# Sample tokens' attention to cached pages, moved from the expert loop to the input projection

## The reference, cut to what matters

```python
p = rmsnorm(x, norm1) @ w_in        # split into q, k, v (attention), q/k/v of the delta rule, z, b, a
q, k = rmsnorm(q), rmsnorm(k)       # 4 heads, 2 parts of 64
s = q . k * 64**-0.5 - slope * |distance|           # masked
w = softmax(s)[part 0] - lam * softmax(s)[part 1]
oa = w @ v                          # prompt: over the prompt; sample: over 1024 cached positions + its own
ob = gated_delta_rule(conv(...))    # 64-token chunks, state carried
x = x + concat(rmsnorm(oa), rmsnorm(ob) * silu(z)) @ w_out
h = rmsnorm(x, norm2); q = h @ peer_wq; choose 16 of 128x128 experts for each of 8 heads
x = x + sum_k gate_k * gelu(h . u[e_k]) * v[e_k]    # 128 expert rows for every token
```

## Time and profile before

| | us |
|---|---|
| three runs | 2112.43, 2114.84, 2120.7 |
| median | 2114.84 |
| the profiled execution | 2114.1 |
| its span, first to last instruction | 2112.3 |
| PE busy | 1779.3 (84%) |
| DVE busy | 1330.4 (63%) |
| ACT busy | 801.4 (38%) |
| POOL busy | 740.7 (35%) |
| DMA | 773.26 MB, mean 366 GB/s |

### The profile page before, as it was taken

How to read it: one execution, slowest core, us unless ns; L and a number is a source line. 1 busy time by engine, 2 the same in 40 slices (tenths; PEclk the granted TensorE clock), 3 DMA queues, 4 the chain that set the end, 5 groups by cost and what they waited for, 6 DMA issues and landing times.

```text
span 2112.3 us, 20529 instructions
## 1 busy us (share of the span) xinstructions
PE 1779.3 (84%) x6195; PEld 885.2 (42%) x6195; DVE 1330.4 (63%) x3021; ACT 801.4 (38%) x2386; POOL 740.7 (35%) x638
## 2 busy tenths in 40 slices
PE   8899999889888798968778897879688799776777
PEld 3345454645344444534444543445233333442111
DVE  2661434489765699766578887567664554569554
ACT  2432222254452356344334646324333322323433
POOL 1210011234444453534434363443322233444442
PEclk9999999999898999989999999979899899989999
DMA  9682312699999999999999999999999999999998
GB/s 306 229 297 75 115 44 90 241 410 426 405 426 428 427 426 426 414 428 407 428 426 426 399 419 422 424 426 427 420 344 412 379 404 393 428 427 427 427 428 334
DMA packets 139817, 773.26 MB, mean 366 GB/s; under 512 B 14641, under 2 KB 23617, under 8 KB 62122
## 3 DMA queue, kind: packets, MB, share of 16 engines
q0 software_dynamic: 83232, 604.52, 68.7%
q1 hardware_dynamic: 52994, 160.12, 20.2%
q10 hardware_dynamic: 3480, 7.31, 1.0%
HBM read 755.91 MB, written 16.26 MB: 366 GB/s over the span
## 4 chain that ended last, share of the span: by engine, by line
PE 42%; DMA 29%; DVE 12%; ACT 8%; issue 5%; POOL 3%; SPq 1%; ACTq 0%; DVEq 0%; POOLq 0%
DMA sb_uv<-in_peer_uv,sb_eidx 23%; PE bank L2061 19%; PE bank L1687 5%; DVE sb_uv L1666 5%; PE bank L2028 3%; PE bank L1962 3%; DMA sb_zone<-in_cache_kT 2%; PE bank L1996 2%; PE bank L1941 2%; POOL sb_uv L906 1%; ACT sb_diag L1263 1%; ACT sb_ew L1256 1%; DMA sb_zone<-in_w_route 1%; POOL sb_brs L849 1%; PE bank L1796 1%
## 5 line engine op out<-in xcount | busy, mean ns | idle before, releaser
L2061 PE MATMUL bank<-sb_uv,sb_diag 128*128 128x512 f32 (+1 forms) x1860 | 942.7, 642 | 250.2 <-ACT sb_diag L1263 239.7
L906 POOL DMA_INDIRECT sb_uv<-in_peer_uv,sb_eidx x576 | 672.8, 1168 | 1010.6 <-PE bank L2061 810.4
L1666 DVE CUSTOM_DVE_ANT_0 sb_uv<-sb_uv,sb_xn 128x1024 f32<-128x1024 f32 x576 | 697.2, 1220 | 282.6 <-DMA sb_uv<-in_peer_uv,sb_eidx 281.3
L2061 PEld LDWEIGHTS bank<-sb_uv,sb_diag 128*128 128x128 f32 (+1 forms) x1860 | 331.1, 193 | 729.4 <-ACT sb_diag L1263 393.5
L1252 ACT ACTIVATE sb_gel<-sb_h 128x1 f32<-128x1 f32 x576 | 116.0, 201 | 796.6 <-DVE sb_h L1666 793.0
L1687 PE MATMUL bank<-sb_w,sb_xnT 128*128 128x512 f32 (+1 forms) x560 | 258.5, 609 | 18.4 <-DVE sb_xnT L1281 8.3
L1263 ACT ACTIVATE sb_diag<-sb_stay,sb_ew 128x128 f32<-128x128 f32 (+1 forms) x465 | 183.2, 394 | 46.5 <-PE bank L2061 2.7
L1640 DVE SCALAR_TENSOR_TENSOR sb_hres<-sb_uv,sb_ew,sb_hres 128x1024 f32<-128x1024 f32 x111 | 142.3, 1282 | 61.4 <-ACT sb_ew L1256 61.3
L1256 ACT ACTIVATE sb_ew<-sb_gel,sb_gate 128x1 f32<-128x1 f32 x576 | 169.6, 294 | 20.3
L2028 PEld LDWEIGHTS bank<-sb_rT,sb_zone 128*128 128x128 f32 x1280 | 156.1, 196 | 28.6 <-issue 28.3
L2028 PE MATMUL bank<-sb_rT,sb_zone 128*128 128x128 f32 x1280 | 157.4, 279 | 2.0 <-issue 1.8
(11 more groups left out here) (321 smaller groups left out, 1528.9 us busy)
## 6 DMA issues: line engine op xcount, KB each, us to landing
sb_zone<-in_w_route SPq DMA_DIRECT2D x20, 2304.0 KB, 12.0
sb_zone<-in_w_mixer SPq DMA_DIRECT2D x10, 2048.0 KB, 12.1
sb_zone<-in_cache_kT SPq DMA_DIRECT2D x64, 256.0 KB, 8.8
sb_zone<-in_cache_v SPq DMA_DIRECT2D x64, 256.0 KB, 15.3
sb_w<-in_w_sections SPq DMA_DIRECT2D x28, 512.0 KB, 5.4
sb_uv<-in_peer_uv,sb_eidx POOLq DMA_INDIRECT x576, 13.6
sb_hres<-pre_conv SPq DMA_DIRECT2D x4, 1024.0 KB
sb_zone<-pre_conv SPq DMA_DIRECT2D x4, 1024.0 KB, 6.2
```

What stands on the lines that cost most here:

```text
L906: nc.gpsimd.indirect_dma_start(uv[:, m % RING, :], None, i["peer_uv"], bass.IndirectOffsetOnAxis(ap=eidx[:, t % 2, n:n + 1], axis=0)).then ...
L1666: nc.vector.tensor_tensor_reduce(out=uv[:, m % RING, 0:D], in0=uv[:, m % RING, 0:D], in1=xn2[:, t % 2, :], scale=1.0, scalar=0.0, op0=ALU. ...
L2061: ins = nc.tensor.matmul(bank[half][0:rows, :], lhsT=G["diag"][:, d % DIAGS, 0:rows], rhs=uv[:, m % RING, D + 512 * half:D + 512 * half + ...
```

## The change

The past attention leaves the expert loop. It now runs between the first units of the projection.

- **Order of units.** `VISITS` starts with the sections v, k, q for tile 4 alone, then come the conv and z sections for all five tiles, then v, k, q for the four prompt tiles. There are still 35 units, but the weights of v, k and q are loaded twice (40 piece loads in place of 28).
- **Place.** `past_at(p, k)` is now 64 + 26 p + k on the scale of the first stage. The units 4 to 14 are due every 10.4, units 15 to 32 every 12.1; `gdn(0)` is due at 182 (was 133), `gdn(1)` at 284 (was 231).
- **Column groups.** Queries are spread over 32 columns for each head, and the four heads write partitions 0, 32, 64 and 96 of one bank; the values go by (half, sequence) to the same four groups; the group changes from one product to the next. The small columns alternate between two groups, with an addition on DVE.
- **Page buffers.** Six quarters of 1 MB: two in the place of the sample states (whose load waits for the last pair), two in `zone`, one in `vtok`, one in `kT`. Keys are issued by SP (`key_loads`), values by POOL (`value_loads`).
- **Other places** for scores, fold matrix, weights and biases; the biases, the tables and the page table are loaded in the first stage; tiles 0 to 3 of the tokens are loaded later (about 29 in place of 0). The norm of the sample outputs (`sample_out_squares`, `sample_out_rstd`, `sample_out_norm`) follows the last pair, and `gdn(0)` waits for it (`s_oa`). In the loop only `mix(PT)` is left for tile 4, with its `w_mixer` load waiting for the scores of tile 3.

```diff
-UNITS = [(g, t) for g in range(NSEC) for t in ORDER]
-Z0, V0, K0 = 3 * NT, 4 * NT, 5 * NT
-LATE = K0 + NT + 3
+VISITS = [(4, [PT]), (5, [PT]), (6, [PT])] + [(g, ORDER) for g in range(4)] + [(g, list(range(PT))) for g in range(4, NSEC)]
+UNITS = [(g, t, v) for v, (g, tiles) in enumerate(VISITS) for t in tiles]
+LAST_OF = [max(n for n, unit in enumerate(UNITS) if unit[2] == v) for v in range(len(VISITS))]
+C0 = 3
+Z0 = C0 + 3 * NT
+V0 = Z0 + NT
...
 def unit_len(n):
-    return 6.9 if n < Z0 else 11.1 if n < LATE else 9.0
+    return 6.9 if n < 4 else 10.4 if n < 15 else 12.1 if n < LATE else 9.0
 
 
 def unit_at(n):
-    if n < Z0:
-        return early_at(22 + 6.9 * n + (10 if n >= NT else 0))
+    if n < 4:
+        return early_at(22 + 6.9 * n)
+    if n < 15:
+        return early_at(55 + 10.4 * (n - 4))
     if n < LATE:
-        return early_at(135 + 11.1 * (n - Z0))
+        return early_at(169.4 + 12.1 * (n - 15))
     return -77 + 9.0 * (n - LATE)
 
...
 def gdn_at(u, k):
     if u < 2:
-        return early_at((133, 231)[u] + (2.06, 2.15)[u] * k)
+        return early_at((182, 284)[u] + (2.06, 2.15)[u] * k)
     return SLOTS * (u - 2) + 11.5 + 0.85 * k
 
...
+    return early_at(64 + 26 * p + k)
 
 
...
+        def load_of(p, values, half, seq):
+            return 8 * p + 4 * values + 2 * half + seq
+
+        def cache_quarter(k):
+
+            b = k % PAGE_BUFFERS
+            if b < 2:
+                return F["sS"][:, 2 * b:2 * b + 2, :, :].rearrange("p h b k -> p (h b k)").rearrange("p (g n) -> p g n", g=4)
+            if b < 4:
...
-                        yield early_at(110 + 9 * h)
+                        yield past_at(NPAIR, 1 + 3 * h)
+                        sp.wait_ge(s_dpv, NPAIR)
                         sp.dma_start(F["sS"][:, h, :, :], i["state_ssm"][0, :, h].rearrange("b v k -> v b k")).then_inc(s_sS, 16)
 
...
-                        n = NT * g - 1
+                    for piece in range(4 * len(VISITS)):
...
-                            sp.wait_ge(s_proj, 4 * n + part - 1)
+                            n, used = LAST_OF[(piece - PIECES) // 4], (piece - PIECES) % 4 + 1
+                            yield unit_at(n) + 0.25 * used * unit_len(n)
+                            sp.wait_ge(s_proj, 4 * n + used)
                         sp.dma_start(F["w"][:, piece % PIECES, :, :].rearrange("p k n -> p (k n)"), i["w_sections"][g][:, quarter_k * part:quarter_k * (part + 1)]).then_inc(s_w[piece % PIECES], 16)
...
+                def key_loads(p):
+                    for half in range(2):
+                        yield (past_at(p - 1, (4.2, 21.5)[half]) if p else early_at(40 + half))
+                        if p == 0:
+                            sp.wait_ge(s_vecs, 112)
+                            sp.wait_ge(s_xnT, 2)
+                        for seq in range(2):
+                            k = load_of(p, 0, half, seq)
+                            pages = []
+                            for g in range(4):
+                                n = (2 * p + seq) * NPG + 4 * half + g
+                                pages.append(sp.value_load(F["pages"][0:1, n:n + 1], min_val=0, max_val=i["cache_kT"].shape[0] - 1))
+                            if p and half == 0:
+                                sp.wait_ge(s_ds, 2 * p)
+                            elif p:
+                                sp.wait_ge(s_dpv, p)
+                            for g in range(4):
+                                sp.dma_start(cache_quarter(k)[:, g, :], i["cache_kT"][bass.ds(pages[g], 1)].rearrange("g p n -> (g p) n")).then_inc(s_keys[half], 16)
 
...
+                def value_loads(p):
+                    for half in range(2):
+                        yield past_at(p, 2.3) if half else past_at(p - 1, 21.6) if p else early_at(42)
+                        if p == 0 and half == 0:
+                            pool.wait_ge(s_vecs, 112)
+                        for seq in range(2):
+                            k = load_of(p, 1, half, seq)
+                            pages = []
+                            for g in range(4):
+                                n = (2 * p + seq) * NPG + 4 * half + g
+                                pages.append(pool.value_load(F["pages"][0:1, n:n + 1], min_val=0, max_val=i["cache_v"].shape[0] - 1))
+                            if half:
+                                pool.wait_ge(s_ds, 2 * p + 1)
+                            elif p:
+                                pool.wait_ge(s_dpv, p)
+                            for g in range(4):
+                                pool.dma_start(cache_quarter(k)[:, g, :], i["cache_v"][bass.ds(pages[g], 1)].rearrange("g p n -> (g p) n")).then_inc(s_vals, 16)
...
+                    for kk in range(0, KC, 2):
+                        for r in range(2):
+                            nc.tensor.matmul(bank[2][32 * r:32 * r + 2 * NH, :], lhsT=F["wba"][:, kk + r, :], rhs=F["xnT"][:, 0:KC * SEQ].rearrange("p (t k r) -> p t k r", t=PT, k=KC)[:, :, kk + r, :], start=kk == 0, stop=kk == KC - 2)
+                        for r in range(2):
+                            ins = nc.tensor.matmul(bank[3][32 * r:32 * r + 2 * NH, 0:LAST], lhsT=F["wba"][:, kk + r, :], rhs=xT(PT)[:, kk + r, :], start=kk == 0, stop=kk == KC - 2)
                     ins.then_inc(s_bap, 1)
-                    yield early_at(75)
...
                 def past(p):
...
+                    for half in range(2):
+                        yield past_at(p, (0, 4)[half])
+                        pe.wait_ge(s_keys[half], 16 + 128 * (p + 1))
+                        if half == 0:
+                            pe.wait_ge(s_qd, 4 * (p + 1))
                             if p:
                                 pe.wait_ge(s_dadd, 4 * p)
+                            else:
+                                pe.wait_ge(s_bad, 2)
+                        for seq in range(2):
+                            for h in range(NH):
+                                ins = nc.tensor.matmul(bank[2 + half][32 * h:32 * h + 32, :].rearrange("p (g k) -> p g k", g=4), lhsT=Qd[:, h, 32 * seq:32 * seq + 32],
+                                                       rhs=cache_quarter(load_of(p, 0, half, seq))[:, :, h * PAGE:(h + 1) * PAGE], start=seq == 0, stop=seq == 1)
                         if half:
...
+                            for seq in range(2):
+                                for h in range(NH):
+                                    ins = nc.tensor.matmul(bank[4][32 * h:32 * h + 32, 0:NSAMP], lhsT=Qd[:, h, 32 * seq:32 * seq + 32], rhs=kT[:, h, NPOS:TOK], start=seq == 0, stop=seq == 1)
                         ins.then_inc(s_ds, 1)
...
+                    yield past_at(p, 15)
                     pe.wait_ge(s_dn, 3 * (p + 1))
                     if p:
                         pe.wait_ge(s_dwc, 2 * p)
+                        pe.wait_ge(s_gatea, 6)
+                    else:
+                        pe.wait_ge(s_bac, 3)
                     for g in range(NPG):
...
+                        nc.tensor.matmul(bank[5][:, 64 * g:64 * g + 64], lhsT=past_S[:, g * PAGE:(g + 1) * PAGE], rhs=past_fold, start=True, stop=True)
+                    nc.tensor.matmul(bank[6][0:NSAMP, 0:64], lhsT=past_S[:, PAST:], rhs=past_fold, start=True, stop=True).then_inc(s_dw, 1)
+                    yield past_at(p, 19.5)
+                    pe.wait_ge(s_dwc, 2 * (p + 1))
+                    if p:
+                        pe.wait_ge(s_doc, p)
+                    pe.wait_ge(s_vals, 256 * (p + 1))
+                    for g in range(4):
+                        for half in range(2):
+                            for seq in range(2):
+                                at = 64 * (4 * half + g) + 32 * seq
+                                r0 = 64 * half + 32 * seq
+                                nc.tensor.matmul(bank[7][r0:r0 + 32, :], lhsT=past_wT[:, at:at + 32], rhs=cache_quarter(load_of(p, 1, half, seq))[:, g, :], start=g == 0, stop=half == 0 and g == 3)
+                    for seq in range(2):
+                        r0 = 64 + 32 * seq
+                        ins = nc.tensor.matmul(bank[7][r0:r0 + 32, :], lhsT=past_wTn[0:NSAMP, 32 * seq:32 * seq + 32], rhs=vtok[0:NSAMP, PT, :], start=False, stop=True)
+                    ins.then_inc(s_dpv, 1)
+                    if p % 2:
+                        yield past_at(p, 26.2)
+                        pe.wait_ge(s_doc, p + 1)
+                        r0 = NSAMP + 32 * (p // 2)
+                        for h in range(NH):
+                            for odd in range(2):
+                                at = 128 * odd + 32 * h
+                                ins = nc.tensor.matmul(bank[6][r0:r0 + 32, h * HD:(h + 1) * HD], lhsT=ea("pick")[:, at:at + 32], rhs=osamp[:, odd, h * HD:(h + 1) * HD], start=odd == 0, stop=odd == 1)
                         ins.then_inc(s_dot, 1)
 ```

555 lines of the change are left out of this document (270 added, 285 removed).

## The result

The changed kernel takes 2131.03 us (median of 10 runs, 2122.24 to 2142.42) against 2114.6 for the kernel before on the same chip: 1.0077 times as long, 95% interval 1.0058 to 1.0096. The prediction was 2080; it missed by 51 us, and by the sign. The profiled execution has a span of 2125.5 us, 13.2 more than before.

The account below looks back on a forecast made before the run. PE was taken to bound the stage before the first gather, the DMA engines the expert loop. From 2114.1 us, 100 less in the loop and 66 more in the first stage (42 + 2 + 22) gave 2080 us, range 2054 to 2108.

Parts of the forecast that it names:

- Part 1: Expert loop, tile 3 to tile 4 output projection: pages and bias tables leave, 433 us become 333, so 100 us go.
- Rival (d): Expert loop: it gives back only the page bytes' 79 us; 2101 us in all, chance 0.03.
- Part 2: PE in the first stage: past attention adds 42 us, with four column groups working side by side at a quarter.
- rival (c): First stage: column groups don't work side by side, 90 us more of PE; 2148 us, chance 0.12.
- Part 3: Gaps at the start of the first stage: idle PE less saved waits for convolution copies, net 2 us, bounds -5 and 10.
- Part 4: DMA engines in the first stage: 201 us of transfers hold `gdn(0)` to 202, 22 us after PE could start it.
- I cost all these at nothing beyond the 22: First stage: units, weight pieces, convolution loads, spills and norm powers standing behind waits add nothing to the DMA term's 22 us.
- Their loss of cover would show in the pair's chain: First stage: spreads, biases, exp and copies on ACT and DVE are hidden; any loss stays within the bound of 48 us.
- rival (b): First stage: waits pile up pair by pair, the DMA term is 48 us and not 22; 2106 us, chance 0.18.
- the pace of 0.11: Sign of being right: eight score or value instructions in a row pace at about 0.11 us and not 0.43.
- the stretch of 333: Sign of being right: the loop's tile-4 stretch falls from 433 to about 333 us at 420 GB/s or more.
- `gdn(0)` at 202: Sign of being right: the transposes of `gdn(0)` in the first stage start at about 202 us.

Follow-up runs that it names:

- groups in the loop: Kernel before, past attention left in the expert loop, the two sequences' products taken in turn, page quarters loaded 0, 2, 1, 3: 2131.1 us, 1.0093 of the kernel before.
- fill runs: Changed kernel with 25 useless products on PE in the places of four waits: 1.0037 and again 1.0039 of the kernel before.
- later fold: Changed kernel with pairs due every 34 us, fold 19.4 in place of 15 after the pair's start, values later too: 2116.5 us, 1.0021 of the kernel before.

## Why the prediction was wrong, step by step

**Bounds of the kernel, Part 1: size right, reason half wrong.** -100 was forecast, -104.5 measured, 96.7 for all behind the first stage. But the dips of the earlier trace rows were put down to PE's serial products; with 52 us fewer of these (groups in the loop) the stretch did not shrink and waits for key pages of 50.3 us stood in it, though that edit changed the order of the loads too. Rival (d) is out.

**Part 2: right.** 42 us were forecast, 40 measured at full clock (44 by the three parts). Four instructions of values start together every 0.43 us:

```profile
101.40 0.59 PE L2049 MATMUL bank<-sb_vtok,sb_zg 128*32 128x512 f32 x1
101.40 0.59 PE L2049 MATMUL bank<-sb_kT,sb_zg 128*32 128x512 f32 x1
101.40 0.60 PE L2049 MATMUL bank<-sb_sS,sb_zg 128*32 128x512 f32 x2
101.83 0.59 PE L2049 MATMUL bank<-sb_vtok,sb_zg 128*32 128x512 f32 x1
```

Against 0.432 us for one instruction that is a factor of 4.0, so rival (c) is out. The Trainium skill ("TensorE: Matmul & The Clock Gate", Measured speedup vs the span model) has 2.38 for three column groups, by which the long products would have cost 7 us more than the sum took. The trace doesn't agree, and the measurement decides: 4.0 for long rows of float32 products over four groups.

**Part 3: too low.** 2 us were forecast; the waits for weight pieces (14.9) and spread queries (5.1), less the 5.7 of the earlier trace rows, are 14. The three sections of weights for one tile each are wanted faster than they land at a DMA share of 0.98.

**Part 4: size right, reason half wrong.** Waits for key pages are 19.7 us for 22. While PE waits for them, the engines are full:

```profile
110.00:120.00 10.00, 7.58 (x29) 2.43 (x27) 2.76 (x5) 4.08 (x15) 4.29 (x8) 1.00 1.02 393
160.00:170.00 10.00, 1.32 (x8) 0.40 (x12) 0.00 (x0) 0.00 (x0) 2.14 (x4) 0.61 1.00 339
210.00:220.00 10.00, 4.98 (x34) 1.59 (x35) 0.84 (x3) 0.64 (x1) 2.14 (x4) 0.67 1.04 401
```

But on the mean they are not: the share is 0.82 from 30 to 200 us, where above 0.9 was forecast, and between the bursts it falls to 0.29 (190 to 200 us). So it isn't the sum of all bytes against PE's time, as the forecast added it up. The pages can be asked for only once the values of the pair before are done (those of pair 1 at 146.5, the key pages of pair 2 issued from 149.2 to 156.2, waited for until 168.7), and then come all at once. A quarter of the bytes took off 20 us, yet left the pairs at 38 us.

**The step that failed: "I cost all these at nothing beyond the 22", with "Their loss of cover would show in the pair's chain".** Two costs stood there. From the last score to the fold 9 to 12 us pass (124.5 to 136.1 for pair 1), and one unit between them is 7: 10.8 us of waits. And waits of all four kinds are followed by work at half clock, most of those of 3 us and more at once: 27 us over the stage. I had seen this in the earlier trace rows and gave it to rival (b) alone; the sum had no term for it. Together with Part 3: 27 + 11 + 12 = 50, less 2 and 2 on Parts 2 and 4 and 2 of small waits that went, 44, which is 109.9 less the forecast 66.

The Trainium skill ("TensorE: Matmul & The Clock Gate", HAM oscillation — how this bites in real kernels) says that a wait for DMA between short bursts of products brings each next burst back to half clock. The trace agrees for the longer waits, 3.64 for 1.92 us, and the fill runs give a price: 4 to 8 us for the waits that they fill.

**Rival (b)** was nearest, but not by its price: 48 us of waits for pages; there were 19.7, and the rest was clock and other waits. Of the signs named, the pace of 0.11 and the stretch of 333 came true, and PE did wait for `cache_kT` once in three of the four pairs; `gdn(0)` at 202 (255), the gather at 477 (521) and the DMA share did not.

Of the 44 us, 7 came back with the later fold and 4 to 8 with the fill. No version gave back all: that the waits and the clock behind them are the whole of the loss is the account of the trace, and the runs confirm it for these parts.

## What to carry to other kernels

When work is moved beside other work on an in-order engine, put down for each chain (score, softmax, fold) its length against the work that lies between its ends, and price a wait on PE with the half clock behind it. Before a wait for a buffer is taken away, ask which one is late next: here waits went from 19.7 to 1.9 us for at most 7 us of time, while 4.4 us more of other work between score and fold gave 7 and useless products in the waits 4 to 8. And before small differences between kernels are read, check in the built programs that their large buffers lie alike modulo 256 bytes; sums of buffer sizes miss the rounding up to 32.
